# Router logits placed between the last projection products, with the second token tile of that group worked by column halves

## The reference

```python
x = x + gla_mixer(rmsnorm(x, c_norm), ...)            # ends in  o @ w_out, w_out 1024 x 1024
x = x + moe_ffn(rmsnorm(x, m_norm), router, w_gate, w_up, w_down)

def moe_ffn(h, router, w_gate, w_up, w_down):
    logits = xt @ router                              # 256 x 1024 times 1024 x 8
    top_v, top_i = lax.top_k(logits, TOP_K)           # TOP_K = 2 of 8 experts for each token
    top_w = jax.nn.softmax(top_v, axis=-1)
    ...
    for e in range(N_EXPERTS):
        out = out + gates[:, e:e+1] * swiglu(xt, w_gate[e], w_up[e], w_down[e])
```

## Time and profile before

| | |
|---|---|
| three runs | 1222.06, 1230.37, 1229.0 us; median 1229.0 |
| profiled execution | 1222.89 us, of which the instructions span 1221.1 us |
| granted TensorE clock, mean of the span | 0.997 |
| PE busy | 1204.9 us, 99% |
| DVE busy | 965.9 us, 79% |
| ACT busy | 815.5 us, 67% |
| DMA | 361.43 MB, mean 296 GB/s |

### The profile page before, as it was taken

One profiled execution on the slowest core, in us unless ns is written; L12 is line 12 of the kernel. 1 busy time (PEld: TensorE's weight loads), 2 busy tenths in 40 slices (PEclk: granted clock), 3 DMA queues, 4 the chain that ended last, 5 costly groups with the idle time before them and its releaser, 6 DMA issues.

```text
span 1221.1 us, 16003 instructions
## 1 busy us (share of the span) xinstructions
PE 1204.9 (99%) x5925; PEld 998.0 (82%) x5928; DVE 965.9 (79%) x935; ACT 815.5 (67%) x879; POOL 60.7 (5%) x89
## 2 busy tenths in 40 slices
PE   8999999999999999999999999999999999999997
PEld 7886888888898878888888888888888888888885
DVE  6977564544657478999899889889989889889896
ACT  7775444343565567777777777777777777777773
POOL 0025000000000000100000000000000000000300
PEclk9999999999999999999999999999999999999999
DMA  9730345544533346999999999999999999999991
GB/s 355 307 138 2 138 172 207 203 171 169 216 138 138 110 183 273 394 382 370 413 372 366 415 365 365 416 370 368 407 371 374 406 366 374 393 364 374 402 421 71
DMA packets 53001, 361.43 MB, mean 296 GB/s; under 512 B 6048, under 2 KB 6560, under 8 KB 10944
## 3 DMA queue, kind: packets, MB, share of 16 engines
q1 hardware_dynamic: 49872, 349.41, 73.9%
q0 software_dynamic: 3056, 11.02, 2.3%
HBM read 354.63 MB, written 5.77 MB: 295 GB/s over the span
## 4 chain that ended last, share of the span: by engine, by line
PE 96%; DVE 1%; ACT 1%; DMA 1%; SPq 0%; issue 0%; DVEq 0%
PE bank L572 29%; PE bank L574 29%; PE bank L573 29%; PE bank L1163 2%; PE bank L1001 1%; PE bank L781 1%; DMA raw<-in_weights 1%; PE bank L796 1%; PE bank L1128 1%; PE bank L817 0%; PE bank L582 0%; PE bank L889 0%; PE bank L1120 0%; ACT hT_hi L1270 0%; PE bank L1022 0%; PE bank L719 0%
## 5 line engine op out<-in xcount | busy, mean ns | idle before, releaser
L2273 DVE TENSOR_TENSOR low<-raw,whi 128x2048 fp32r<-128x2048 f32 x260 | 594.8, 2291 | 66.5 <-ACT whi L1589 59.2
L1589 ACT CAST whi<-raw 128x2048 fp32r<-128x2048 f32 x260 | 497.3, 1913 | 112.8 <-PE bank L574 112.0
L572 PE MATMUL bank<-whi,hT_hi 128*128 128x512 f32 (+1 forms) x1104 | 431.1, 391 | 0.6 <-DVE low L1658 0.3
L574 PE MATMUL bank<-whi,hT_lo 128*128 128x512 f32 (+1 forms) x1104 | 428.7, 388 | 0.0
L573 PE MATMUL bank<-low,hT_hi 128*128 128x512 f32 (+1 forms) x1104 | 428.1, 388 | 0.0
L572 PEld LDWEIGHTS bank<-whi,hT_hi 128*128 128x128 f32 x1104 | 207.3, 188 | 43.6 <-DVE low L1658 0.7
L574 PEld LDWEIGHTS bank<-whi,hT_lo 128*128 128x128 f32 x1104 | 207.3, 188 | 42.7
L573 PEld LDWEIGHTS bank<-low,hT_hi 128*128 128x128 f32 x1104 | 207.4, 188 | 41.6
L1658 DVE TENSOR_TENSOR low<-raw,whi 128x2048 fp32r<-128x2048 f32 x66 | 150.7, 2289 | 44.9 <-ACT whi L1255 44.8
L572 PE MATMUL bank<-whi,h_hi 128*128 128x512 f32 x440 | 181.1, 411 | 0.0
L574 PE MATMUL bank<-whi,h_lo 128*128 128x512 f32 x440 | 172.5, 392 | 0.0
(11 more groups left out here) (320 smaller groups left out, 770.3 us busy)
## 6 DMA issues: line engine op xcount, KB each, us to landing
raw<-in_weights SPq DMA_DIRECT2D x327, 1024.0 KB, 5.9
sums<-ybuf POOLq DMA_DIRECT2D x7, 512.0 KB, 7.2
arena<-in_compress SPq DMA_DIRECT2D x1, 1088.0 KB, 15.0
x<-in_x SPq DMA_DIRECT2D x2, 512.0 KB, 5.2
raw<-in_weights SPq DMA_DIRECT2D x4, 256.0 KB, 5.7
raw<-in_weights SPq DMA_DIRECT2D x2, 512.0 KB, 7.6
tokens<-hng POOLq DMA_DIRECT2D x2, 512.0 KB, 8.8
out<-x SPq DMA_DIRECT2D x4, 256.0 KB, 3.0
```

The costliest lines, as they stand in the source:

```text
L572: mm(out_, a_hi, b_hi, start=start, stop=False)
L574: return mm(out_, a_lo, b_hi, start=False, stop=stop)
L1589: nc.scalar.copy(whi[:, u % SPLIT, :, :], raw[:, u % RAW, :, :]).then_inc(S["w_hi"], 1)
L2273: V.tensor_tensor(low[:, u % RAW, :, :], raw[:, u % RAW, :, :], whi[:, u % SPLIT, :, :].bitcast(F32), ALU.subtract).then_inc(S["w_lo"], 1)
```

## The change

The last group is written out (`last_group`) instead of calling `by_tile`. Tile 0 is as before, 8 k x 3 matmuls of 512 columns. Tile 1 is done in two column halves of 256, each with its own bank and its own 8 k x 3 matmuls: i = 0 for columns 512 to 767 of x, i = 1 for columns 768 to 1023. DVE adds each half on its own (`last_rows`), PE turns each in two blocks (`rows_part`), ACT copies each (`part_turned`), and the matmuls of tile 1's logits are in three parts (k 0 to 3, 4 and 5, 6 and 7). All of tile 0's logits and the first two parts of tile 1's now stand between products of i = 1; the turning of the first twelve blocks stands at k = 2 of i = 0. The sum of squares of tile 1 is split in 768 and 256 columns, and POOL adds the two. `keep_busy` is moved and its counts changed (before 4 and 4, now 2, 2, 3 and 3). `units_used` of the group's first unit is now given behind k = 3 of i = 1.

```diff
--- before.py
+++ after.py
@@ -174,6 +174,7 @@
         sml = sb("sml", [P, R_END])
         wa2 = sb("wa2", [32, 512])
         ss = sb("ss", [P, NT])
+        ss_last = sb("ss_last", [P, 1])
         rstd = sb("rstd", [P, NT])
         mhalf = sb("mhalf", [P, 32])
         esc = sb("esc", [P, 2, 512])
@@ -530,7 +531,9 @@
                 inv_root(ors[:, t * GH:(t + 1) * GH], oss[:, t * GH:(t + 1) * GH], 256, GH, "gla_rstd")
             pool.wait_ge(S["mixed"], NT * GH)
             nc.gpsimd.dma_start(norm_row, row_d[:, :]).then_inc(S["norm_row"], 16)
-            norm(3)
+            pool.wait_ge(S["ss"], NT * 4 + 1)
+            link(nc.gpsimd.tensor_tensor(ss[:, 1:2], ss[:, 1:2], ss_last[:, :], ALU.add))
+            inv_root(rstd[:], ss[:], DM, NT, "rstd")
             pool.wait_ge(S["rows"], NT)
             for t in range(NT):
                 nc.gpsimd.dma_start(tokens_d[t * P:(t + 1) * P, :], hng[:, t, :]).then_inc(S["tokens_out"], 16)
@@ -1072,37 +1075,75 @@
                 transposes(x, 5, 0, lambda half: pe.wait_ge(S["x_ready"], 8 + 1 + 2 * half))
                 transposes(x, 5, 1, lambda half: pe.wait_ge(S["x_ready"], 8 + 2), (0,))
 
-            def logits_by_expert(half):
-
-                pe.wait_ge(S["rows_T"], half + 1)
-                for k in range(4 * half, 4 * half + 4):
-                    last = mm(bank[4][0:NE, 0:P], router[:, k, :], rows_T[0][:, k, :],
-                              start=(k == 0), stop=(k == NK - 1))
-                if half:
-                    last.then_inc(S["logits_T"], 1)
-
-            def logits_by_token(half):
-
-                pe.wait_ge(S["rows_T"], 2 + half + 1)
-                for k in range(4 * half, 4 * half + 4):
+            def rows_part(i):
+
+                for j in range(2):
+                    k = 4 + 2 * i + j
+                    last = nc.tensor.transpose(bank[PART_BANKS[i]][:, j * P:(j + 1) * P], x[:, 1, k * P:(k + 1) * P], ident)
+                last.then_inc(S["hT_psum"], 1)
+
+            def logits_by_expert():
+
+                pe.wait_ge(S["router"], 1)
+                pe.wait_ge(S["rows_T"], 2)
+                for k in range(NK):
+                    last = mm(bank[4][0:NE, 0:P], router[:, k, :], rows_T[0][:, k, :], start=(k == 0), stop=(k == NK - 1))
+                last.then_inc(S["logits_T"], 1)
+
+            def logits_by_token(part):
+
+                pe.wait_ge(S["rows_T"], 3 + part)
+                for k in ((0, 1, 2, 3), (4, 5), (6, 7))[part]:
                     last = mm(bank[6][:, 0:NE], rows_T[1][:, k, :], router[:, k, :],
                               start=(k == 0), stop=(k == NK - 1))
-                if half:
+                if part == 2:
                     last.then_inc(S["logits"], 1)
 
-            by_tile(U_C_OUT, 1, C_OUT_BANKS[1], None, {(1, 2): early_rows})
-            pe.wait_ge(S["router"], 1)
-            logits_by_expert(0)
-            transposes(x, 5, 1, lambda half: pe.wait_ge(S["x_ready"], 8 + 4), (1,))
-            logits_by_expert(1)
-            logits_by_token(0)
-            pe.wait_ge(S["logits_row"], 1)
-            nc.tensor.transpose(bank[4][:, 2 * P:2 * P + NE], logits_row, ident[0:NE, 0:NE]).then_inc(S["logits"], 1)
-            logits_by_token(1)
-            keep_busy(4, 5)
+            def first_half_turned():
+
+                pe.wait_ge(S["x_half"], 1)
+                rows_part(0)
+
+            def first_logits_turned():
+
+                pe.wait_ge(S["logits_row"], 1)
+                nc.tensor.transpose(bank[4][:, 2 * P:2 * P + NE], logits_row, ident[0:NE, 0:NE]).then_inc(S["logits"], 1)
+
+            def last_group():
+
+                hooks = {(0, 2): early_rows, (1, 0): logits_by_expert, (1, 1): lambda: logits_by_token(0),
+                         (1, 2): first_half_turned, (1, 4): first_logits_turned, (1, 6): lambda: logits_by_token(1)}
+                for k in range(NK):
+                    b = NK + k
+                    if b % UB == 0:
+                        pe.wait_ge(S["w_lo"], U_C_OUT + b // UB + 1)
+                    w_h, w_l = block_at(U_C_OUT, b)
+                    last = mm3(bank[C_OUT_BANKS[1][0]][:, :], hT_hi[:, k, 0:P], hT_lo[:, k, 0:P], w_h, w_l,
+                               k == 0, k == NK - 1)
+                last.then_inc(S["tile0"], 1)
+                for i in range(2):
+                    for k in range(NK):
+                        if (i, k) in hooks:
+                            hooks[i, k]()
+                        b, c = NK + k, slice(i * CH, (i + 1) * CH)
+                        w_h, w_l = block_at(U_C_OUT, b)
+                        last = mm3(bank[LAST_BANKS[i]][:, 0:CH], hT_hi[:, k, P:2 * P], hT_lo[:, k, P:2 * P],
+                                   w_h[:, c], w_l[:, c], k == 0, k == NK - 1)
+                        if i and b % UB == UB - 1:
+                            last.then_inc(S["units_used"], 1)
+                    if i == 0:
+                        last.then_inc(S["tile0"], 1)
+
+            last_group()
+            keep_busy(2, 0)
+            pe.wait_ge(S["x_ready"], 8 + 4)
+            rows_part(1)
+            keep_busy(2, 0)
+            logits_by_token(2)
             pe.wait_ge(S["picked"], 1)
             mm(bank[1][:, 0:8], tri, picked[:, 0, :], start=True, stop=True)
             mm(bank[1][:, 8:16], ones, picked[:, 0, :], start=True, stop=False)
+            keep_busy(3, 5)
             pe.wait_ge(S["picked"], 2)
             mm(bank[1][:, 8:16], tri, picked[:, 1, :], start=False, stop=True).then_inc(S["rank"], 1)
             mm(bank[2][:, 0:8], ones, picked[:, 0, :], start=True, stop=False)
@@ -1548,8 +1589,19 @@
             rows_turned(1, 0)
             norm(3, 0)
             split(U_MOE + 2)
-            rows_turned(1, 1)
-            norm(3, 1)
+            act.wait_ge(S["x_half"], 1)
+            A(hn[:, 1, 0:3 * CH], x[:, 1, 0:3 * CH], ACT.Square, accum_out=ss[:, 1:2]).then_inc(S["ss"], 1)
+
+            def part_turned(i):
+
+                act.wait_ge(S["hT_psum"], in_psum(5, 1, 1) + i)
+                nc.scalar.copy(rows_T[1][:, 4 + 2 * i:6 + 2 * i, :],
+                               bank[PART_BANKS[i]][:, 0:2 * P].rearrange("p (k n) -> p k n", k=2)).then_inc(S["rows_T"], 1)
+
+            part_turned(0)
+            act.wait_ge(S["x_ready"], 8 + 4)
+            A(hn[:, 1, 3 * CH:DM], x[:, 1, 3 * CH:DM], ACT.Square, accum_out=ss_last[:, :]).then_inc(S["ss"], 1)
+            part_turned(1)
             split(U_MOE + 3)
             act.wait_ge(S["gap"], 1)
             A(ee, ee, ACT.Exp).then_inc(S["gap_exp"], 1)
@@ -2140,8 +2192,14 @@
 
             dve.wait_ge(S["norm_row"], 16)
             weighted(0)
-            residual(U_C_OUT, 1, 1, C_OUT_BANKS, 6)
-            weighted(1)
+
+            def last_rows(i, ready):
+
+                xs = x[:, 1, BLK + i * CH:BLK + (i + 1) * CH]
+                V.tensor_tensor(xs, xs, bank[LAST_BANKS[i]][:, 0:CH], ALU.add).then_inc(S[ready], 1)
+
+            dve.wait_ge(S["tile0"], 7)
+            last_rows(0, "x_half")
             dve.wait_ge(S["logits_T"], 1)
             V.tensor_copy(logits_row, bank[4][0:NE, 0:P]).then_inc(S["logits_row"], 1)
             link(V.memset(slot[:, :, :], -1.0))
@@ -2156,6 +2214,9 @@
                 V.tensor_tensor(picked[:, t, :], oh[:, 0, t, :], oh[:, 1, t, :], ALU.add).then_inc(S["picked"], 1)
 
             chosen(0)
+            dve.wait_ge(S["units_used"], U_C_OUT + 4)
+            last_rows(1, "x_ready")
+            weighted(1)
             chosen(1)
             dve.wait_ge(S["picked"], 2)
             V.tensor_scalar(unseen.unsqueeze(2), picked[:, :, 0:1], -4.0 * SEQ, 4.0 * SEQ - 1.0, ALU.mult, ALU.add)
@@ -2425,6 +2486,7 @@
 A_OUT_BANKS, C_OUT_BANKS = ((6, 7), (4, 5)), ((6, 4), (7, 5))
 
 LEVEL_BANKS = (6, 7, 4, 5, 6, 7, 4, 5)
+PART_BANKS, LAST_BANKS = (0, 3), (5, 1)
 DRAIN_BANKS = (6, 7, 0, 1)
 GLA_BANKS = (6, 7, 4, 5)
 SCORE_BANKS = ((0, 1), (6, 7))
```

2 lines of the change are left out of this document (1 added, 1 removed).

## The result

The changed kernel's median is 1233.37 us (21 runs, 1231.24 to 1238.32), against 1229.26 for the kernel before beside it (21 runs, 1222.06 to 1233.72): ratio 1.0043, 95% interval 1.0029 to 1.0057. The forecast was 1232.6, in 1224.0 to 1236.5. The sum for the routing came close, and the total did too, but the total for a reason that isn't in the forecast: two terms of 6 to 8 us that I had not seen, one up and one down, nearly cancel each other.

What follows compares the result with a forecast made beforehand. PE, busy 99% of the span, was taken as the bound. Group +7.0 us (0.3 narrower products, 4.2 moved in, 2.5 wait), 4.4 won behind it, 1.0 clock: +3.6 on 1229.0 gives 1232.6 us, range 1224.0 to 1236.5.

Steps and rivals of the forecast that it cites:

- The wait at k = 6: In i = 1 of tile 1, PE waits for ACT's copy of the first two turned blocks: 2.5 us idle.
- The narrower products: In tile 1 of the last group, 48 matmuls of 256 columns for 24 of 512: +0.30 us.
- Behind the group at full clock: From the last group to the first expert product: 8.2 us instead of 12.6, 4.4 won.
- POOL's added sum: Behind the group, POOL adds tile 1's two sums of squares: some 0.2 us, with rstd not late.
- The clock: Around the routing, one stretch of 3.4 us at 1.2 GHz again, somewhere from 454 to 462, costing 1.0 us.
- the long one: Rival: a second slow stretch covers the dispatch and the first expert products, +6 to +8 us, 1235 to 1237; chance 0.18.
- the clock staying up: Rival: wait present but no slow stretch in the routing, +2.6 us, 1231.6; chance 0.13.
- The kernel before's own drop: 3.4 us at 1.2 GHz, costing about 1.0 us in fillers ahead of the dispatch and 1.0 in the dispatch.
- Up to which the two kernels are the same: Until tile 1 of the last group starts at 443.43 us, both kernels were taken as equal; times were carried on from there.
- as long as the stretch behind it stays filled: An edit is worth the shift of the first expert's first product, provided PE's work behind that stays filled.
- What separates them is not in the trace and I take it as unchanged: The kernel before's runs, 1222.06, 1229.0 and 1230.4 us, differ for an unseen reason, assumed unchanged; 1229.0 is the base.
- The chances by the 1% bound: Whole kernel: faster by over 1% (12.3 us) 0.02, within 0.95, slower by over 1% 0.03.

Runs made afterwards that it cites:

- e1: Changed kernel with ACT's split of U_MOE + 2 moved behind the copy of the first two turned blocks; 1229.99 us, ratio 1.0022 to the kernel before.
- e2: Changed kernel with nine 512-column fillers ahead of the wait at k = 6, the wait kept; 1232.55 us, ratio 1.0041 to the kernel before.
- e10: Kernel before with only tile 1's products in two column halves, all logits behind the group; 1221.56 us, ratio 0.9959.
- e6: Changed kernel with ACT's copy ahead of its split and no address moved; 1222.32 us, ratio 0.9936 to the kernel before.
- c_after: Changed kernel once more, unaltered; 1234.94 us, ratio 1.0059 to the kernel before.
- e5: Changed kernel with ss_last kept in an existing pad tensor so that no address moves; 1227.50 us, ratio 0.9977 to the kernel before.
- c_before: Kernel before once more, unaltered, for a second trace; 1228.11 us, ratio 0.9980.
- e4: Kernel before with an unused 4-byte tensor (32 bytes allocated) where the change puts ss_last; 1232.82 us, ratio 1.0036.
- e8: Kernel before with an unused tensor of 64 bytes where the change puts ss_last; 1236.93 us, ratio 1.0054.
- e9: Kernel before with an unused tensor of 128 bytes where the change puts ss_last; 1235.69 us, ratio 1.0061.
- e7: Kernel before with 26 more PE instructions, waits on a semaphore already at its value, at the start; 1224.16 us, ratio 0.9954.

## Why the prediction was right, and where it wasn't

**The wait at k = 6: right, by its own steps.** Times from tile 1's start: PE reached k = 6 at 9.8 us (forecast 10.0), ACT's split began at 9.0 (9.2), the copy was there at 12.0 (12.3 without the 0.2 of handing over), and PE was idle 2.1 us (2.5), 2.3 by e1 against e2. The last product began at 13.2 (13.6). The narrower products cost 0.36 us (e10) where I had 0.30.

**Behind the group at full clock: right.** 8.20 us in e1, e2 and e6 each, forecast 8.2. The sum of both, 22.0, is 21.4 in e2. POOL's added sum took 0.68 us where I had 0.2, and rstd came at 461.7, 1.0 us before DVE first read it (462.7), so it cost nothing.

**The clock: mis-sized.** The step was "I expect one stretch of 3.4 us at 1.2 GHz again ... I take 1.0". No execution that was profiled shows that: the low stretch is 10.2 us (13.7 in c_after) and costs 4.2, or there is none. In the runs of the kernel after the two clumps lie 3.5 us apart (medians 1233.05 and 1236.55). I had the long one as a rival at 0.18, the clock staying up at 0.13; the long one came in 8 of 21 runs, and in the 13 others the mean clock (0.998 to 0.999) says that it stayed up or nearly so. The cause of the long one is the idle time at k = 6 with small matmuls behind it: with PE filled there (e2) or not waiting (e1) none of 24 runs had it; e5, which keeps the wait, had it in 6 of 12 (1228.8 to 1230.0, the others 1224.8 to 1226.3). Why it was 10.2 us in two profiles and 13.7 in the third stays open. The kernel before's own drop wasn't fixed either: c_before, e4 and e8 show none, and their routing is 1.65 us shorter (17.7 against 19.4), where I had 2.0 for it; e9 has it for 6.8 us and takes 21.0, with no idle time in PE.

**"Up to which the two kernels are the same" and "as long as the stretch behind it stays filled": failed.** The stretch stayed filled and still took longer. A tensor of 4 bytes moved the operands of the experts and of the trunk, and the mean distance of the products there grew by 1%: +6.3 us in the experts and +1.4 to +1.9 before the last group in the profiles, 5.9 to 7.4 in the medians (e5), shown from both sides (e4 has the cost without the change, e5 the change without the cost). I had costed what the change does with instructions and nothing of what it does with addresses.

**"What separates them is not in the trace and I take it as unchanged": failed.** The base 1229.0 held the long tail of part of the executions, and neither profile of the changed kernel has it. e7's median is 5.1 to 6.5 us lower, and 6.6 to 8.6 without its own waits at the start.

**The sum.** The routing alone, with addresses and code length equal, is e5 against e7, and e7's waits at the start (445.51 - 443.81 = 1.7 us) have to be taken off: 1227.50 - (1224.16 - 1.7) = +5.0 us, where I had +3.6. The address costs 1233.37 - 1227.50 = +5.9, the tail gives 1224.16 - 1.7 - 1229.26 = -6.8. These add up to the measured +4.1 by necessity, since they are that difference taken apart in three steps; only the parts say something, and they are uncertain by the 2.7 us by which the chips differ in the kernel before. So the mechanism of the forecast stands, its size was some 1.4 us too small, since half of e5's runs have the long low stretch, and that its total came within 0.8 us of the median is luck in good part: with one of the two unseen terms alone it would have been off by 5 or more. The chances by the 1% bound held.

## What to carry to other kernels

When work is put between other work, follow each wait back on the engine that feeds it: the mark that frees a buffer moved too, and the copy queued behind the split came 2 us late; one line, the copy ahead of the split, takes that away, though the order without it is still no faster than the old one. Compare kernels only with their tensors in the same places and their programs of like length, or measure both by themselves (an unused tensor, some idle instructions), before a difference under 1% is put down to an edit. Idle instructions cost time themselves, and that has to be read from the trace and taken off. And look at how the runs scatter, not only at their median: two clumps can be two mechanisms, and a profile shows one of them.

## What the runs showed of the hardware

- Where operands lie in the on-chip memory changes the rate of matmuls that are otherwise equal: 512-column products stood 0.2274 us apart in the mean, and 0.2296, 0.2291 and 0.2284 after a shift by 32, 64 and 128 bytes, with PE busy and the granted clock at 1.00. The median distance stayed 0.227; what changed is how many products came late. The rule behind these numbers stays open.
- The end of a program can take 7.6 us more with two more instruction fetches (52 against 50, c_before against before), 5.9 of them in one branch. With 26 more instructions on PE, which do nothing, neither e7's profile nor its band of runs shows them; those instructions cost 1.5 to 2.1 us at the start.
- The clock fell to 1.2 GHz without idle time, amid small matmuls, for 3.4 us (before, e7) and 6.8 us (e9), and in other executions of such kernels not at all (c_before, e4, e8). With 2.1 us of idle time ahead (after, c_after, e5) it fell for 10.2 to 13.7 us in the three that were profiled, and by time and mean clock in 19 of 43 runs, in the other 24 hardly. The Trainium skill, page "TensorE: Matmul & The Clock Gate", section "HAM oscillation — how this bites in real kernels", warns of idle gaps in PE's work. e1 and e2 go with that, since without a gap none of 24 runs had the long fall; the gaps of its example are longer than the 2.1 us here, and the kernel before's own fall in a row of small matmuls had no gap at all.
- Adding two columns of 128 x 1 on GpSimd took 0.68 us, nearly as much as its step on 128 x 2 with `mhalf` (0.71).
